# Sample attention: step 0's values ahead of step 1's scores, and step 1's values requested directly behind step 1's keys

## The reference

```python
k_a = jnp.concatenate([pk_a, a_k], axis=1)      # cached pages, then the new keys
...
# moba_attention
gate = jnp.einsum('bchd,bhnd->bhcn', qc.astype(jnp.float32), k_mean)
_, top_i = lax.top_k(jnp.where(past, gate, NEG_INF), n_sel)        # 3 of 4 past blocks
...
s = jnp.einsum('bchd,bhcskd->bhcsk', qc, kg).astype(jnp.float32) * scale
p = masked_softmax(s.reshape(B, MOBA_HEADS, C, -1), mask.reshape(B, MOBA_HEADS, C, -1))
o = jnp.einsum('bhcsk,bhcskd->bchd', p.reshape(s.shape).astype(vg.dtype), vg)
...
# nsa_attention: compressed keys, 16 of 17 chosen blocks, and a window
p_c = masked_softmax(s_c, cmp_end[None, :] <= pc[:, None])
imp = jnp.einsum('bgrcn,nj->bgcj', p_c, overlap)
_, top_i = lax.top_k(imp, n_top)
p_s = masked_softmax(s_s..., mask_s...)
p_w = masked_softmax(s_w, mask_w)
o = jnp.stack([o_c, o_s, o_w], axis=-2)
```

## Time and profile before

| | |
|---|---|
| time, median of 3 runs | 922.28 us (920.47 to 923.59) |
| profiled execution | 921.98 us, span 920.2 us |
| TensorE matmuls, busy | 766.7 us (83%) |
| TensorE weight loads, busy | 426.6 us (46%) |
| VectorE, busy | 259.9 us (28%) |
| ScalarE, busy | 163.4 us (18%) |
| GpSimd, busy | 81.5 us (9%) |
| bytes moved by DMA | 238.57 MB, 259 GB/s on average |
| chain that ended last | TensorE 67%, DMA 19%, VectorE 7% |

### The profile page before, as it was taken

One profiled execution on the slowest core, in us unless ns is written; L12 is line 12 of the kernel. 1 busy time (PEld: TensorE's weight loads), 2 busy tenths in 40 slices (PEclk: granted clock), 3 DMA queues, 4 the chain that ended last, 5 costly groups with the idle time before them and its releaser, 6 DMA issues.

```text
span 920.2 us, 10780 instructions
## 1 busy us (share of the span) xinstructions
PE 766.7 (83%) x3964; PEld 426.6 (46%) x3964; DVE 259.9 (28%) x792; ACT 163.4 (18%) x401; POOL 81.5 (9%) x119
## 2 busy tenths in 40 slices
PE   2999999999999775987789986389987987876585
PEld 2636665555666542443456655233322322322184
DVE  0223332011000886555512235611111011111005
ACT  2013432111001662222200021011111010110002
POOL 0000000032000342000000000111101001001000
PEclk9999999999999898978899996579999989998756
DMA  9968678252440675799998432148999999986041
GB/s 358 395 212 296 239 274 295 118 226 92 183 183 0 219 286 191 266 346 388 351 411 382 183 132 77 33 174 332 425 422 423 423 423 423 424 334 259 13 104 57
DMA packets 51369, 238.57 MB, mean 259 GB/s; under 512 B 8930, under 2 KB 17122, under 8 KB 39090
## 3 DMA queue, kind: packets, MB, share of 16 engines
q1 hardware_dynamic: 42834, 223.93, 62.2%
q0 software_dynamic: 6176, 11.83, 3.7%
q10 hardware_dynamic: 2304, 2.10, 0.7%
HBM read 236.43 MB, written 18.09 MB: 277 GB/s over the span
## 4 chain that ended last, share of the span: by engine, by line
PE 67%; DMA 19%; DVE 7%; issue 3%; SPq 1%; ACT 1%; POOL 0%; POOLq 0%; DVEq 0%; ACTq 0%
PE bank L484 15%; DMA arena<-in_w_ein 15%; PE bank L845 8%; PE bank L457 6%; PE bank L778 4%; PE bank L787 4%; PE bank L865 4%; PE bank L894 3%; PE bank L440 2%; PE bank L527 2%; DMA arena<-in_w_br 2%; PE bank L681 2%; PE bank L492 1%; DMA arena<-in_w 1%; PE bank L834 1%
## 5 line engine op out<-in xcount | busy, mean ns | idle before, releaser
L845 PE MATMUL bank<-arena 128*64 128x512 f32 x544 | 138.1, 666 | 33.1 <-DMA arena<-in_w_ein 31.3
L484 PE MATMUL bank<-arena 128*128 128x320 f32 x512 | 141.7, 433 | 0.0
L484 PEld LDWEIGHTS bank<-arena 128*128 128x128 f32 x512 | 95.7, 189 | 45.3 <-issue 6.4
L845 PEld LDWEIGHTS bank<-arena 128*64 128x64 f32 x544 | 42.1, 152 | 118.1 <-issue 84.5
L865 PE MATMUL bank<-arena 128*64 128x512 f32 x272 | 62.1, 598 | 1.4 <-issue 1.4
L1637 DVE COPY arena<-bank 128x512 f32<-128x512 f32 x17 | 11.8, 692 | 162.3 <-PE bank L834 162.3
L457 PE MATMUL bank<-arena 128*128 128x512 f32 x128 | 56.8, 594 | 0.0
L1101 ACT ACTIVATE arena<-bank 128x256 f32<-128x256 f32 x17 | 6.5, 385 | 180.0 <-PE bank L845 180.0
L1760 POOL DMA_INDIRECT y_rows<-arena,rows_of_slots_out x17 | 17.1, 1004 | 231.7 <-DVE arena L1651 231.7
L778 PE MATMUL bank<-arena 128*128 128x320 f32 x128 | 36.5, 447 | 1.3 <-DMA arena<-in_w_br 1.3
L457 PEld LDWEIGHTS bank<-arena 128*128 128x128 f32 x128 | 23.4, 187 | 28.5 <-issue 27.5
(11 more groups left out here) (312 smaller groups left out, 888.9 us busy)
## 6 DMA issues: line engine op xcount, KB each, us to landing
arena<-in_w_ein SPq DMA_DIRECT2D x16, 4096.0 KB, 34.2
arena<-in_w_eout SPq DMA_DIRECT2D x16, 2048.0 KB, 24.8
arena<-in_w_ada SPq DMA_DIRECT2D x12, 2048.0 KB, 9.3
arena<-in_w_in SPq DMA_DIRECT2D x10, 2048.0 KB, 9.9
arena<-in_k_pages SPq DMA_DIRECT2D x64, 320.0 KB, 6.3
arena<-in_v_pages SPq DMA_DIRECT2D x64, 320.0 KB, 9.8
arena<-in_cmp_pages SPq DMA_DIRECT2D x48, 128.0 KB, 9.2
arena<-in_win SPq DMA_DIRECT2D x16, 256.0 KB, 5.0
```

What stands on the lines that cost most here:

```text
L484: m = mm(banks[c % 4][:, 0:N], ring[q][:, k, P * (c % 4):P * (c % 4 + 1)], hT[:, k, :], start=(k == 0), stop=(k == KD - 1))
L845: m = mm(banks[2 + p % 2][CAP * e:CAP * (e + 1), :], xeT[p % 2][:, k, CAP * e:CAP * (e + 1)], wi2[p % 3][:, e, k, :], start=(k == 0), stop ...
```

## The change

Two places are edited. On TensorE `smp_values(0)` is called right behind `smp_turn(0)`, ahead of `smp_scores(1)`; for steps 1 to 3 the order is the old one. On SyncE the order of requests becomes: keys 0, values 0, numbers 1, keys 1, values 1, numbers 2, keys 2, numbers 3, keys 3, values 2, values 3, branch weights. The waits stay attached to the same requests.

```diff
             keys(1)
-            for i in range(1, 4):
-                later = page_ids(i + 1) if i < 3 else None
-                if i < 3:
-                    ids[(i + 1) % 2] = later
-                    keys(i + 1)
-                values(i)
+            values(1)
+            ids[0] = page_ids(2)
+            keys(2)
+            ids[1] = page_ids(3)
+            keys(3)
+            values(2)
+            values(3)
             sp.wait_ge(z_kd[1], 4)
...
                 smp_turn(i)
+                if i == 0:
+                    smp_values(0)
                 if i + 1 < 4:
                     smp_scores(i + 1)
-                smp_values(i)
+                if i:
+                    smp_values(i)
                 if i + 1 < 4:
                     smp_group(i + 1)
```

## The result

The changed kernel takes 932.93 us (median of 4 runs, 929.82 to 938.09) against 922.93 us for the kernel before (4 runs, 920.47 to 924.48). The ratio is 1.0116 with a 95% interval of 1.0062 to 1.0170: slower by 10.7 us by the ratio, 10.0 between the medians. The forecast was 931.0 us in a range of 926.8 to 934.2, with 0.92 for slower.

The account below looks back on a forecast made before the run. TensorE's chain through the sample attention to the branch weights was taken as the bound; late keys and the low clock end step 2's scores 8.7 us later, 921.98 + 8.7 = 930.7, or 931.0 at the median, range 926.8 to 934.2.

Parts of the forecast that it names:

- Chosen part: VectorE's work for step 1 after the blocks and step 0's rows out: starts at 394.7, against 389.70 before.
- Second part of turning: TensorE's later turning of step 1's probabilities, behind VectorE's work and the exponential: at 401.2, against 396.27 before.
- TensorE's order: Step 0's values ahead of step 1's scores leave VectorE's 5.03 us on blocks uncovered: 4.9 us once.
- Value requests: SyncE's 18 requests for step 1's values: start at 377.2, take 11.45 us, end at 388.6, between 387.8 and 389.9.
- Numbers: SyncE's reading of step 2's 16 page numbers, now in full view before step 2's keys: 9.2 us.
- Landing of the keys: Step 2's keys, requested at 397.8: first half there 9.95 us later at 407.8, second 16.55 us later at 414.4.
- the wait for the first half: TensorE wants step 2's scores at 405.0 and waits for their keys to 407.8: 2.8 us.
- The clock: TensorE's 1.2 GHz level in the first half of step 2's scores: adds 0 to 2.7 us.
- all moves together: After step 2's scores, 8.7 us late, everything behind shifts by one amount; no slack takes it up.
- rival 1: Step 2's keys come in time and only TensorE's changed order costs: 4.9 us, 927.2; 0.15 with what lies between.
- rival 2: TensorE's low clock stays through all of step 2's scores: 12.7 us later, 935.0; chance 0.11.
- rival 3: Transfers bound the stage and the change fills a 6.3 us hole in them: faster, 916.0; chance 0.04.

Follow-up runs that it names:

- numbers_first: The changed kernel with step 2's page numbers read ahead of step 1's value requests instead of behind them: 930.79 us, ratio 1.0100 to the kernel before.
- numbers_late: The kernel before with one added wait, so SyncE reads step 2's page numbers only at the keys_used count: 932.60 us, ratio 1.0102.
- te_only: The kernel before with only TensorE's order changed, step 0's values ahead of step 1's scores, requests as before: 934.45 us, ratio 1.0108.

## Why the prediction was right

The steps, with what the profile shows in the time of before (0.6 us taken off):

- Values of step 0 start at 372.9: 373.0. Scores of step 1 at 381.8: 381.9. VectorE's blocks at 388.6: 388.7. Chosen part at 394.7: 394.7. Second part of turning at 401.2: 401.3. TensorE's order costs 5.0 us once, as forecast (4.9).
- Value requests at 377.2: 377.3. They took 10.3 us, not 11.45: this term was 1.2 us too large and lies outside the ends that I kept for it by 0.3.
- Numbers 9.2 us: 9.2. numbers_first takes them out of view and the wait with them.
- Landing of the keys: mis-sized. I took 9.95 us and 16.55 us from the flow of step 1's bytes; TensorE was released 11.4 and 19.0 us after the first request. A window in which the bytes have flown is not yet the count that the waiting engine sees: the last page took 9.68 us from request to landing.
- These two errors point opposite ways. That the wait for the first half, forecast at 2.8 us, came out at 2.96 is in part luck.
- A second wait, 0.34 us before the second half, came too; the prediction had said that the first would be the only one.
- The clock: between nothing and 2.7 us, half of it taken. It was 2.5 (7.3 us less 4.78), in the second profile 2.0. It set nothing: at full clock the first half would have ended sooner, and the second would still have begun when its keys were there, at 415.7 in the time of before and not at 414.4. That late landing alone puts the end of the scores at 418.6 instead of 417.5.
- Behind it "all moves together": nearly. Of the 10.4 us of the stage 9.8 stand by step 2's turning; the last 0.6 are mostly scores at the low level again, those of step 3 (8.36 us against 7.87). The branch projection starts 10.1 us later (481.32, so 480.72, against 470.61).

The result is 10.0 us between the medians, 10.7 by the ratio, for a forecast of 8.7: the mechanism was as forecast, and 1.1 us of what is missing is the landing of the second half of the keys. The rivals: keys in time (rival 1) is what numbers_first comes near to, and it needs an edit; the low clock through all of the scores (rival 2) held for the first half only; the transfers as the bound (rival 3) fell, the value requests came at 377.3 in the time of before, behind the hole in the transfers, as the row of 377.2 had said.

What I had not seen is why the two halves belong together. With TensorE's order alone, step 2's values come 3.3 to 4.3 us late; the new order of requests takes that away and pays with step 2's keys, 3.3 us of waiting, or more at full clock, where the low level in their first half would turn into waiting. Set against each other the new requests gain nothing: the stage is 110.7 and 110.6 us with them, and without them 111.8 and 116.3, or 108.7 and 110.0 with the clock's excess in the values taken off.

## What to carry to other kernels

Before a block of work is put ahead of another, list what each of the two covers on the other engines: here the values covered 5 us of VectorE's blocks, which stood bare once the values came first. A request stream with waits in it is one queue for everything behind it: count the reading of addresses as part of it (0.58 us each here), and place it where a wait hides it. Take the time to landing from the engine that was released, not from the flow of bytes.

## What the runs showed that I had not expected

- 16 page numbers read at the wrong place cost 7.9 us of their 9.2 in numbers_late, where the keys behind them had slack for all but 0.6 us: the values behind the keys had none.
- The last 0.15 MB of some 5.8 MB took 2.46 us, from 413.86 to TensorE's start at 416.32, while the first 5.64 MB flowed at 341 GB/s.
- te_only ran step 0's values at the 1.2 GHz level in both of its profiles, 11.97 and 11.84 us for 8.91, behind the same instructions as kernels that ran them at full clock.
